# One block for all stages of a two-layer hybrid decoder, and the routers, norms and sort split by token half and by step

## The chip, the cores and the metric

The kernel runs on one core of one Trainium2 chip, as one launch. The metric is the device time of that launch in microseconds (us); lower is better. Everything is float32. Engines in the profile: PE (TensorE, with PEld for its weight loads), DVE (VectorE), ACT (ScalarE), POOL (GpSimd), SP (SyncE, which issues all DMAs; SPq is its DMA issuing).

## The reference

The input x has 256 tokens of 1024 features. Two layers, each a mixer and a mixture of experts (MoE), and a last RMSNorm:

```
h = x
for layer in 0, 1:
    u = rms_norm(h, norm_mix[layer])
    h = h + (RWKV-7 heads and sparse attention, if layer 0; Mamba-2 mixer, if layer 1)(u)
    h = h + hier_moe(rms_norm(h, norm_ffn[layer]))
return rms_norm(h, norm_final)

def hier_moe(t):                                # t: 256 x 1024
    pg = softmax(t @ wg + bg)                   # 4 groups, the best one is taken
    le = t @ we + be                            # 8 experts in each group
    e_val, e_idx = top_k(softmax(le of the group), 2)
    comb = weights of the two experts, times pg of the group
    return sum over 32 experts of comb_e * ((silu(t @ w_gate_e) * (t @ w_up_e)) @ w_down_e)
```

Each of the 32 experts has three matrices of 1024 x 512 (2 MB each). A token uses two experts, but all 32 are needed, so a layer reads 192 MB of weights.

## The kernel before, in words

`build` emits five `nc.Block`s in a row: "hyb" (mixer of layer 0), experts of layer 0, "ssm" (mixer of layer 1), experts of layer 1, "final". At the end of a block every engine waits for the others. Inside a block the engines run their own programs, written out by hand in order, and meet by counting semaphores: `then_inc(..., X.one(mark))` sets a mark and `wait_ge(*at(mark))` waits for it. `take` hands out PSUM banks in turn from a named pool and makes PE wait until the last user of that bank has been read (mark `"read", job`).

**Weights.** `raw` is a ring of 24 slots of 8 KB per partition, each holding one chunk of 1 MB: six per expert (gate and up in halves 0 to 3, down in 4 and 5). `load_ahead` (L383) issues chunks 0 to 23 as soon as the mixer's buffers that lie in the same memory are free; `main_sync` (L1762) issues the other 168, each when the chunk 24 before it has been used (semaphore `used`). Most go as whole matrices of 2 MB (`load_matrix`, L378). The first four experts are fixed to numbers 0 to 3. The order of the others comes from a sort of the experts by their token counts (`sort`, L1877, four rounds of 8 on DVE): SP waits for `order` before chunk 24 and reads the expert's number from `seq`.

**Mixer buffers.** The Areas `hyb` and `mam` lay the mixers' tensors over the ring in the order in which they come free. `hyb_fed` to `hyb_half` and `mam_projected` to `mam_left` count the slots that are free at a stage. In layer 0 they are 2, 6, 12 and 16; in layer 1 8, 12, 15, 17 and 22. The last two slots hold `hg_`, `uT_` and `junk_` of the router, and so are loaded last.

**Join.** At the end of a mixer PE multiplies its output with the output projection into four banks (two token halves t, two column halves c), and DVE adds each to h. In "hyb" (L1561 to L1578) PE does the attention part for all four tiles, then for each t transposes `mixr` (`turnr`), waits until ACT has copied it to `srcr`, and does the scan part. In "ssm" it is `joined(g)` for four groups (L2777).

**Router** (`router_sync`, `router_act`, `router_pe`, `router_dve`, L1609 to L1717). `norm_act` squares and sums h and takes the root (a table load for Exp comes behind it), `norm_dve` multiplies by the gain and builds `diag`, the identity times 1/std. PE opens the four accumulator banks with h (L1638), turns the weighted h by 16 matmuls against `diag` (`turn_pe`, L272), and once all are copied to `uT_` it computes the logits (L1647, 8 matmuls over 256 columns, 64 outputs). ACT adds the bias and writes `lgT`, PE folds it back to tokens (L1652), and three matmuls with the identity follow (L1656). DVE finds the best group and the two best experts (L1686 to L1709, `hit`), PE ranks each token within its expert and counts (L1659 to L1664), and DVE copies `rank`.

**Experts.** `select_fixed` (L1861) builds one-hot matrices for the first four experts in two operations (equal to rank, times hit), `weights_dve` and `weigh` the combine weights. Then `counts_dve` and `sort`. PE gathers the tokens (`gather_fixed`, L1968), and for each expert: project (L2014), turn, silu, down (L2052), scatter into the accumulators (L2061). A quarter of `used` is counted behind each half of project and each half of down.

**Mixer of layer 1.** `norm_act` and `norm_dve` read the accumulators `sums` in the order t = 1, 0; four matmuls with the identity run on PE; then turning (L272), copies (L281), projections (L2655, `project(n, j)`), pairs of heads (`pair`), sums of squares (`total(g)`, read by `root(g)`, L2568), all taking banks from one pool of eight. **Final** is the same norm and two outputs of 512 KB.

## Time and profile before

| | us |
|---|---|
| median of 3 runs | 1376.61 |
| lowest and highest | 1375.62, 1377.4 |
| span of the profiled execution | 1369.6 |
| its PE busy | 1239.2 (90%) |
| its DVE busy | 406.1 (30%) |
| its ACT busy | 268.7 (20%) |
| HBM read | 461.51 MB |

The span runs from the first to the last instruction of one profiled execution; the median is the device time of launches. Times in the rows count from the start of the span. PE is counted busy while matmuls are in its pipeline, also where it goes slowly, and its share is an average over stages with different limits. Stages of layer 0: mixer to 230, router to 253, experts to 678. Layer 1: mixer to 912, router to 937, experts to 1361, then the end.

### The profile page before, as it was taken

What the parts mean: (1) busy time and instruction counts of PE and PEld (TensorE: products, weight loads), DVE (VectorE), ACT (ScalarE), POOL (GpSimd) and SP (SyncE); (2) the same over time, 40 slices, a digit from 0 to 9 for tenths busy, and PEclk for the clock granted to TensorE, in tenths of its full rate; (3) what the DMA queues carried; (4) which work ended last, traced back from release to release, by engine and by line L of the source; (5) the groups of instructions that cost most, each with busy time, mean ns of one, the idle gap of its engine ahead of it and who ended that gap; (6) DMA issues with size and microseconds to landing.
All of it is one profiled execution on the core that took longest, in us unless ns stands there. A gap on an engine that the chain in (4) does not pass through costs nothing. (4 is left out here: it accounts for less than half of the span.)

```text
span 1369.6 us, 20884 instructions
## 1 busy us (share of the span) xinstructions
PE 1239.2 (90%) x8796; PEld 685.6 (50%) x8796; DVE 406.1 (30%) x1017; ACT 268.7 (20%) x537; POOL 25.5 (2%) x22
## 2 busy tenths in 40 slices
PE   6999989899999887698999999988999998877986
PEld 3678754444444333344388888444444443333432
DVE  1158963421211111021236757224212111210211
ACT  2241532110110100010222566011101100000101
POOL 0000300000000000000000011000000000000000
PEclk9999999999999999799999999999999999987999
DMA  9630158999999999999944473958999999999996
GB/s 305 193 112 13 65 218 352 405 428 428 427 427 428 427 427 427 426 426 427 361 152 169 156 277 142 418 230 328 427 428 427 427 428 427 428 427 425 428 427 260
DMA packets 63482, 464.08 MB, mean 339 GB/s; under 512 B 8272, under 2 KB 13680, under 8 KB 34960
## 3 DMA queue, kind: packets, MB, share of 16 engines
q1 hardware_dynamic: 63376, 462.61, 82.6%
q8 instruction: 73, 1.20, 0.4%
q14 instruction: 33, 0.27, 0.1%
HBM read 461.51 MB, written 1.08 MB: 338 GB/s over the span
## 5 line engine op out<-in xcount | busy, mean ns | idle before, releaser
L2014 PE MATMUL bank<-raw,xg 128*32 128x512 f32 x1664 | 234.1, 654 | 46.3 <-DMA raw<-in_moe_w_up 40.9
L1924 DVE TENSOR_TENSOR aT<-bank,sg 128x128 f32<-128x128 f32 (+1 forms) x64 | 20.2, 316 | 553.5 <-ACT sg L1835 553.5
L2014 PEld LDWEIGHTS bank<-raw,xg 128*32 128x32 f32 x1664 | 59.1, 118 | 195.6 <-issue 118.9
L1951 PE MATMUL bank<-sel,ux 128*128 128x64 f32 (+1 forms) x896 | 117.7, 287 | 17.3 <-DVE sel L1857 16.4
L1951 PEld LDWEIGHTS bank<-sel,ux 128*128 128x128 f32 x896 | 110.9, 202 | 41.0 <-issue 21.6
L2061 PE MATMUL sums<-ys,selT 64*128 64x512 f32 x512 | 127.2, 615 | 3.3 <-DVE ys L1937 3.3
L1832 ACT COPY gus<-bank 128x512 f32<-128x512 f32 x64 | 37.5, 585 | 439.4 <-PE bank L2014 331.8
L2052 PE MATMUL bank<-raw,aT 128*32 128x512 f32 x832 | 101.7, 607 | 10.7 <-DVE aT L1924 10.7
L2061 PEld LDWEIGHTS sums<-ys,selT 64*128 64x128 f32 x512 | 44.0, 186 | 88.0 <-issue 80.4
L1995 PE MATMUL bank<-raw,xg 128*64 128x512 f32 x384 | 87.3, 594 | 0.0
L2655 PE MATMUL sums<-uT,wr 128*128 128x256 f32 x352 | 78.1, 380 | 0.0
L1937 DVE COPY ys<-bank 128x512 f32<-128x512 f32 x64 | 44.0, 688 | 113.3 <-PE bank L2052 81.5
L2025 PEld LDWEIGHTS bank<-cst,gus 128*128 128x128 f32 x416 | 50.3, 191 | 44.5 <-issue 34.9
L2655 PEld LDWEIGHTS sums<-uT,wr 128*128 128x128 f32 x352 | 66.3, 190 | 9.4 <-issue 0.7
L2025 PE MATMUL bank<-cst,gus 128*128 128x64 f32 x416 | 57.5, 281 | 4.2 <-ACT gus L1832 4.2
L1806 ACT COPY xg<-bank 128x256 f32<-128x256 f32 (+1 forms) x56 | 23.4, 418 | 178.3 <-PE bank L1951 178.3
L2655 PE MATMUL bank<-uT,wr 128*128 128x256 f32 x256 | 57.1, 381 | 0.0
L1995 PEld LDWEIGHTS bank<-raw,xg 128*64 128x64 f32 x384 | 30.2, 137 | 51.5 <-issue 48.7
L2655 PEld LDWEIGHTS bank<-uT,wr 128*128 128x128 f32 x256 | 48.0, 190 | 6.9 <-issue 0.7
L2052 PEld LDWEIGHTS bank<-raw,aT 128*32 128x32 f32 x832 | 21.9, 110 | 51.3 <-issue 30.8
L2039 PE MATMUL bank<-raw,aT 128*64 128x512 f32 x192 | 43.8, 598 | 3.0 <-DVE aT L1924 3.0
L1835 ACT ACTIVATE sg<-bank 128x128 f32<-128x128 f32 (+1 forms) x64 | 19.0, 297 | 137.8 <-PE bank L2025 114.8
(419 smaller groups left out, 1260.8 us busy)
## 6 DMA issues: line engine op xcount, KB each, us to landing
raw<-in_moe_w_gate SPq DMA_DIRECT2D x54, 2048.0 KB, 41.7
raw<-in_moe_w_up SPq DMA_DIRECT2D x54, 2048.0 KB, 46.1
raw<-in_moe_w_down SPq DMA_DIRECT2D x54, 2048.0 KB, 44.7
raw<-in_moe_w_gate SPq DMA_DIRECT2D x20, 1024.0 KB, 11.6
raw<-in_moe_w_up SPq DMA_DIRECT2D x20, 1024.0 KB, 12.6
raw<-in_moe_w_down SPq DMA_DIRECT2D x20, 1024.0 KB, 12.3
wr<-in_ssm_w_in SPq DMA_DIRECT2D x10, 2048.0 KB, 8.0
wr<-in_hyb_w_in SPq DMA_DIRECT2D x5, 2048.0 KB, 7.8
```

The lines of the kernel that those rows point to most:

```text
L1806: nc.scalar.copy(dst[:, :, 4 * half:4 * half + 4, :].rearrange("p x k s -> p k x s"), bank[SIDE_BANK][:, 0:8 * n].rearrange("p (k x s) -> ...
L1832: nc.scalar.copy(gus[:, :, :], bank[GU_BANK][:, :].rearrange("p (q j) -> p j q", j=4)).then_inc(S["gus"], 1)
L1924: V.tensor_tensor(out, bank[TURN_BANK][:, 0:8 * n].rearrange("p (j x) -> p j x", j=4)[:, :, n:2 * n], gated, ALU.mult).then_inc(S["act"], 1)
L1937: V.tensor_copy(ys[:, :], bank[Y_BANK][:, :]).then_inc(S["y"], 1)
L1951: i = T.matmul(bank[SIDE_BANK][:, k * n:(k + 1) * n].rearrange("p (x s) -> p x s", x=2), ux[:, t, 4 * half + k, :], src[:, t, :, :], start ...
L1995: i = T.matmul(bank[GU_BANK][CAP * m:CAP * m + CAP, :], xg[:, odd, k, :], raw[:, slot, (k % 4) * FH:(k % 4 + 1) * FH], start=(k == 0), sto ...
L2014: i = T.matmul(bank[GU_BANK][CAP_S * c:CAP_S * c + CAP_S, :], xg_f[:, x, 4 * half + k, :], raw[:, slot, k * FH:(k + 1) * FH], start=(half ...
L2025: i = T.matmul(bank[TURN_BANK][:, j * CAP:(j + 1) * CAP], gus[:, j, :], C("ident64"), start=True, stop=True)
L2039: i = T.matmul(bank[Y_BANK][CAP * n:CAP * n + CAP, :], aT[:, j, :], raw[:, slot, jj * D + n * BANK:jj * D + (n + 1) * BANK], start=(j == 0 ...
L2052: i = T.matmul(bank[Y_BANK][CAP_S * c:CAP_S * c + CAP_S, :], aT_s[:, 2 * half + jj, :], raw[:, slot, jj * D + n * BANK:jj * D + (n + 1) * ...
L2061: i = T.matmul(bank[ACC[2 * t + n]][:, :], selT[CAP * n:CAP * n + CAP, x, t * P:(t + 1) * P], ys[CAP * n:CAP * n + CAP, :], start=False, s ...
L2655: i = T.matmul(b[:, c * SEQ:(c + 1) * SEQ], wr2[:, n % 3, k, (2 * j + c) * P:(2 * j + c + 1) * P], uT2[:, k, :], start=(k == 0), stop=(k = ...
```

## The change

1. **One block.** The five blocks become one ("all"); all waits between stages are now marks. SP's first wait of the router is for the last join tile, and of the mixer of layer 1 for the last scatter.
2. **Join.** Attention's part is done tile by tile and interleaved with the transposes of `mixr`; the `wj` weights come in one DMA. The adds to h move into the router's DVE program and write to `hn(t)`, in slot 22. The first token half is transposed (`turn_h`, plain transposes of the h that isn't normed yet) ahead of the last tile's matmuls. So in both layers.
3. **Router.** Squares in halves of 512 columns, by tile. The gain is multiplied into `rw` once by POOL (`router_weighted`), the bias is a row `rbias`, and 1/std and the bias are applied to the folded logits (`lg`) in one DVE operation per half. Logits in two groups of 128 columns. `ux` is computed from `hn` in one operation with factor and gain. The openings of the accumulators move: three between fold and rank, where the three identity matmuls were, the fourth behind rank and count, ahead of the gather. The Exp table is loaded behind the copies of `lgT`.
4. **Selection.** The table `before` has -1024 on its diagonal, so that a token not in an expert has a rank that fits no slot; `select_fixed` reads rank from PSUM in one operation per half, and `rank` is copied after it. `rexp` is waited for later, by ACT.
5. **Sort.** Two rounds, then the order of experts 4 to 15 (first count of `order`), then the weights, then the other two rounds (second count, awaited by SP before expert 16), then the overflow test.
6. **Buffers.** The first mixer's are laid out by last reading: `wr` becomes `even` and `odd`. The slots free at a stage are now 2, 4 (`hyb_scored`, behind POOL's `gain`), 7, 14 and 19. In layer 1 slot 18 is loaded when `joined(1)` is done, 15 to 17 when `joined(2)` is, and 19 to 21 at the join's end. In both layers slot 23 follows the logits, and slot 22 `ux` and the last opening.
7. **Norm into the mixer and at the end** (`sums_act`, `sums_weighted`): in halves of 512 columns, t = 0 first; the last scatter frees token half 0 by itself. Two instead of four identity matmuls. The last output of half 1 goes in two pieces, scaled by DVE and ACT.
8. **Banks at the end of the mixer of layer 1.** `project(9, ...)`, `pair(13)` to `pair(15)` and `total(2)`, `total(3)` take the four accumulator banks, the join the other four.

The diff, cut to its core:

```diff
+    entire = ExitStack()
+    block = entire.enter_context(nc.Block(name="all", no_gpsimd_drain=True))
...
-    put("before", (i[:, None] < i[None, :]).astype(np.float32))
+    put("before", (i[:, None] < i[None, :]) - MISS * np.eye(P))
...
+    def sums_act(act, tag, junk, ss, part, std):
+        for t in range(HALVES):
+            act.wait_ge(*at("h", tag, t))
+            square_act(act, sums[:, t, side(1)], junk, ss, 2 * t, "sq", tag, t, 1)
+            mean_act(act, ss, 2 * t, part, t)
+            act.wait_ge(*at("hg", tag, t, 0))
+            square_act(act, sums[:, t, side(0)], junk, ss, 2 * t + 1, "sq", tag, t, 0)
+            root_act(act, tag, ss, 2 * t + 1, part, std, t)
...
+    def turn_h(pe, tag, t, q):
+        b = take(pe, "turn", tag, t, q, pool=FREE)
+        pe.wait_ge(*at("h", tag, t, q))
+        for k in range(4):
+            i = nc.tensor.transpose(b[:, k * P:(k + 1) * P], hn(t)[:, (4 * q + k) * P:(4 * q + k + 1) * P], C("ident"))
+        i.then_inc(pe_done, PE.one(("turn", tag, t, q)))
...
+    def router_weighted(pool, layer):
+        pool.wait_ge(s_ld["rw"], 32 * (layer + 1))
+        nc.gpsimd.tensor_tensor(rw[:, :, :], rw[:, :, :], rep(FT(f"ffn{layer}"), LW, 2), ALU.mult).then_inc(
+            pool_done, PO.one(("rw", layer)))
...
+        attention_joined(0, 0)
+        attention_joined(0, 1)
+        attention_joined(1, 0)
+        scan_turned(0)
+        attention_joined(1, 1)
+        scan_turned(1)
+        pe.wait_ge(s_ld["wj"], 16)
+        scan_joined(0, 0)
+        scan_joined(0, 1)
+        scan_joined(1, 0)
+        turn_h(pe, "ffn0", 0, 0)
+        turn_h(pe, "ffn0", 0, 1)
+        scan_joined(1, 1)
...
         def router_sync(sp):
+            sp.wait_ge(*at("join", name, 1, 1))
             load_ahead(sp, layer, ahead[layer], NSLOT - 2)
+            sp.wait_ge(*at("logits", tag, 1))
+            load_ahead(sp, layer, NSLOT - 1, NSLOT)
             sp.wait_ge(*at("uhi", tag, 1))
-            sp.wait_ge(*at("logits", tag))
-            load_ahead(sp, layer, NSLOT - 2, NSLOT)
+            sp.wait_ge(*at("opened", tag))
+            load_ahead(sp, layer, NSLOT - 2, NSLOT - 1)
...
         def router_pe(pe):
+            turn_h(pe, tag, 1, 0)
+            turn_h(pe, tag, 1, 1)
+            pe.wait_ge(*at("rw", layer))
...
-                i = T.matmul(b[lo:lo + LW, 0:SEQ], rw[:, k, :], uT_[:, k, :], start=(k < 2), stop=(k >= KD - 2))
+                    i = T.matmul(b[lo:lo + LW, 0:P], rw[:, k, :], uT_[:, k, t * P:(t + 1) * P], start=(k < 2),
+                                 stop=(k >= KD - 2))
...
-            for j in range(3):
-                T.matmul(bank[GU_BANK][:, :], C("ident"), cst[:, 0:BANK], start=True, stop=True)
+            opened(0, 0)
+            opened(0, 1)
+            opened(1, 0)
             pe.wait_ge(*at("hit", tag))
...
+            opened(1, 1).then_inc(pe_done, PE.one(("opened", tag)))
...
+                go(V.scalar_tensor_tensor(out=lg[:, t, :], in0=bank_of("folded", tag)[:, t * LG:(t + 1) * LG],
+                                          scalar=rstd_[:, t:t + 1], in1=rbias[:, :], op0=ALU.mult, op1=ALU.add),
...
                     if s == FIXED:
-                        sp.wait_ge(ps.s["order"], layer + 1)
+                        sp.wait_ge(ps.s["order"], 2 * layer + 1)
+                    elif s == MIXED:
+                        sp.wait_ge(ps.s["order"], 2 * layer + 2)
...
                 select_fixed()
+                ranked_dve(dve)
+                counts_dve(dve)
+                sort(range(2))
+                order_mixed()
                 weights_dve(dve)
                 weigh(ids, plan[0] == "S")
-                counts_dve(dve)
-                sort()
+                sort(range(2, EXPERTS // 8))
+                order_small()
+                overflow()
...
-        for j in range(4):
+        for j in range(2):
             T.matmul(bank[SIDE_BANK][:, :], ident, cst[:, 0:BANK], start=True, stop=True)
...
+        project(9, 0, ACC)
+        pair(13, ACC)
+        pair(14, ACC)
+        project(9, 1, ACC)
+        pair(15, ACC)
+        total(2, ACC)
```

## Rows read from the trace of the kernel before

**Rows 1.** The page: DMA busy tenths and GB/s, 40 slices of 34.24 us

```profile
DMA  9630158999999999999944473958999999999996
GB/s 305 193 112 13 65 218 352 405 428 428 427 427 428 427 427 427 426 426 427 361 152 169 156 277 142 418 230 328 427 428 427 427 428 427 428 427 425 428 427 260
```

**Rows 2.** Stretches A:B, engines' busy us and counts, PEclk, DMA share, GB/s

```profile
core 0: us, PE busy (x) PEld busy (x) DVE busy (x) ACT busy (x) POOL busy (x), PEclk, DMA share, GB/s
250.00:253.15 3.15, 2.69 (x28) 1.65 (x24) 2.71 (x20) 0.53 (x2) 0.00 (x0) 1.00 0.99 411
300.00:400.00 100.00, 98.76 (x612) 45.12 (x604) 15.52 (x42) 11.04 (x24) 0.00 (x0) 1.00 1.01 427
670.00:674.00 4.00, 3.31 (x20) 1.36 (x23) 0.29 (x1) 1.76 (x3) 0.00 (x0) 0.70 0.43 141
690.00:837.70 147.70, 144.81 (x751) 122.11 (x750) 86.80 (x208) 70.20 (x94) 13.01 (x12) 1.00 0.50 179
```

**Rows 3.** Timeline, join of layer 0: start, us, engine, line, operation, [idle, releaser]

```profile
197.69 11.95 PE L1567 MATMUL bank<-zz,qk 128*128 128x512 f32 x24
...
212.92 0.60 PE L1173 MATMUL sums<-cst,mixr 128*128 128x128 f32 x4
213.55 0.58 ACT L1133 COPY dcy<-sums 128x512 f32<-128x512 f32 x1 [9.84 <-PE sums L1173]
...
229.61 0.69 DVE L908 TENSOR_TENSOR h<-bank,h 128x512 f32<-128x512 f32 x1 [2.74 <-PE bank L1576]
```

**Rows 4.** Timeline, router of layer 0 up to the first resumed weight load

```profile
234.21 3.73 PE L272 MATMUL bank<-diag,hg 128*128 128x128 f32 x32
...
238.67 1.95 PE L1647 MATMUL bank<-uT,rw 128*64 128x256 f32 x16 [0.72 <-issue]
240.65 0.47 ACT L1623 ACTIVATE lgT<-bank,feat 128x256 f32<-128x256 f32 x1 [2.08 <-PE bank L1647]
...
241.85 0.25 DVE L1686 MAX8 top<-bank 128x8 f32<-128x8 f32 x2 [5.22 <-PE bank L1652]
...
244.33 0.22 DVE L1709 TENSOR_TENSOR hit<-hits 128x64 f32<-128x64 f32 x1
...
244.60 0.43 PE L1659 MATMUL bank<-hit,cst 128*128 128x64 f32 x2
...
246.06 0.43 DVE L1865 TENSOR_TENSOR sel<-sel,hit 128x256 f32<-128x256 f32 x1
...
246.64 2.47 PE L1968 MATMUL bank<-sel,ux 128*128 128x128 f32 x20 [0.95 <-DVE hits L1727]
...
249.12 1.92 PE L2014 MATMUL bank<-raw,xg 128*32 128x512 f32 x16
...
251.99 0.17 DVE L1893 CAST seq<-ranked 128x16 int32<-128x16 uint32 x1
...
253.15 0.36 SPq L380 DMA_DIRECT2D raw<-in_moe_w_gate  x1
```

**Rows 5.** Timeline, layer 1: last join add, first resumed weight load

```profile
912.00 0.69 DVE L2511 TENSOR_TENSOR h<-sums,h 128x512 f32<-128x512 f32 x1 [2.74 <-PE sums L2784]
...
937.28 0.34 SPq L380 DMA_DIRECT2D raw<-in_moe_w_gate  x1
```

**Rows 6.** Timeline, end of layer 0 and start of the mixer of layer 1

```profile
676.00 1.99 PE L2061 MATMUL sums<-ys,selT 64*128 64x512 f32 x8 [0.82 <-DVE ys L1937]
...
682.11 3.78 PE L272 MATMUL bank<-diag,front 128*128 128x128 f32 x32
...
686.62 0.67 PE L2708 MATMUL sums<-uT,wr 128*128 128x256 f32 x2 [0.72 <-issue]
```

**Rows 7.** Timeline, late mixer: project(9, 0) on PE and root(1) on ACT

```profile
838.25 7.07 PE L2655 MATMUL sums<-uT,wr 128*128 128x256 f32 x32
838.45 0.47 ACT L2568 ACTIVATE rs<-sums,eps_n 128x256 f32<-128x256 f32 x1 [0.43 <-PE sums L2692]
```

**Rows 8.** Timeline, final norm and output, in a span of 1369.6

```profile
1361.23 1.02 ACT L232 ACTIVATE junk_f<-sums 128x1024 f32<-128x1024 f32 x1 [4.18 <-PEq L2125]
...
1365.12 1.20 SPq L295 DMA_DIRECT2D out<-o_f  x2
```

More of the change, by code:

```diff
@@ L1349, in _, with against @@
+        by_channels(5, NV, 0)
+        scores(1)
+        def against(name, left_):
+            for t in range(HALVES):
+                bs = [take(pe, name, t, e, pool=right) for e in range(2)]
                 for c in range(4):
@@ new lines, in _ @@
+                        if t == 1 and c == 3 and q == 1:
+                            i.then_inc(pe_done, PE.one(("nn", e)))
+        by_channels(5, NV, 1)
+        weights_turned(0)
+        pe.wait_ge(*at("rt"))
+        against("bar", bh)
+        bs = [take(pe, "crossed", e, pool=right) for e in range(2)]
+        for c in range(4):
+            for e in range(2):
+                for q in range(2):
+                    i = T.matmul(bs[e][at64(1 - q), c * CHK:(c + 1) * CHK],
+                                 bh[at64(e), c, chunk(1, q)], ar[at64(e), c, 0, chunk(1, q)], start=True, stop=True)
@@ new lines, in _, with products @@
+        straight = lambda g, q: q
+        crossed = lambda g, q: q if g == 0 else 1 - q
+        def products(l):
+            pe.wait_ge(*at("lvl", l))
+            if l == 1:
+                pe.wait_ge(*at("triT0"))
+            else:
+                pe.wait_ge(*at("read", "dT", l - 1, 1))
+            bs = {g: take(pe, "prod", l, g, pool=right) for g in range(2)}
+            squares(bs, lv[:, l % 2], tri, straight, crossed).then_inc(pe_done, PE.one(("prod", l, 1)))
+            new[("prod", l, 0)] = new[("prod", l, 1)]
@@ new lines, in _ @@
+        pe.wait_ge(*at("read", "dTT", LAST, 1))
+        for e in range(2):
+            bs = [take(pe, "wu", t, e, pool=right) for t in range(HALVES)]
+            for c in range(4):
+                for q in range(2):
+                    for t in range(HALVES):
+                        half = at64(crossed(t, q))
+                        i = T.matmul(bs[t][at64(q), 2 * c * CHK:2 * (c + 1) * CHK], triT[half, slot(t, e, c), :],
+                                     flat(xr_[half, slot(t, e, c), :, :], "x", "s"), start=True, stop=True)
+            i.then_inc(pe_done, PE.one(("wu", 1, e)))
+            new[("wu", 0, e)] = new[("wu", 1, e)]
@@ L1447, in _, with within @@
+        def within(t):
+            b = take(pe, "y", t, pool=right)
             for e in range(2):
```

3131 lines of the change are left out of this document (1581 added, 1550 removed).

## The prediction

> **What bounds the kernel now.** I read the page's row of slices first. The DMA engines are full in two long stretches, at 425 to 428 GB/s [rows 1], and in each the kernel streams the expert weights of one layer. A layer has 192 chunks of 1,048,576 bytes. The ring holds 24, so 168 chunks (176.2 MB) can start only once slots are freed: 412 us at 427 GB/s [rows 2]. In the stretch 300 to 400 us PE is 98.8% busy, but so is the DMA, and what PE does faster only empties the ring earlier. So the end of a layer is fixed by the moment at which the stream resumes after the first 24 chunks, plus about 420 us. That moment is the DMA issue at 253.15 in layer 0 and at 937.28 in layer 1 [rows 4, 5]. Whatever lies ahead of it counts fully; whatever lies behind it is hidden.
>
> The second reading is the timeline from the last output projection ("join") to that issue. In layer 0 the last add to h starts at 229.61, so I call J = 229.57 the end of the join on PE [rows 3]; the stream resumes 23.6 us later. In layer 1 J is 911.96 [rows 5] and the distance 25.3 us. These two stretches are serial chains: block change, norm, 16 turning matmuls, logits, bias, fold, picking of experts, rank, select, gather, first half of an expert [rows 4]. The DMA is still busy at 250 to 253 in layer 0 at nearly full rate [rows 2], so there the chunk loads finish only just ahead of the issue: a shorter router alone would soon hit them.
>
> Third, the mixer of layer 1 is PE's: 144.8 of 147.7 us busy at clock 1.00 [rows 2]. It takes as long as it did, moved earlier as a whole. Fourth, the end: norm and output, serial [rows 8].
>
> **The change, part by part.**
>
> *Join of layer 0.* Before, PE waited twice for a copy out of PSUM between transposing mixr and using it: four transposes from 212.92, then the copy of 0.58 at 213.55 [rows 3], about 0.65 in which PE has nothing. Now attention's and scan's matmuls are interleaved, and others cover both waits: -1.3. Two groups of raw transposes for the router (four take 0.60 [rows 3], about 0.5 back to back) are put ahead of the last output tile: +1.0. The 32 matmuls of 512 columns and the transposes of mixr stay. J comes at 229.3, 0.3 earlier; bounds 1.3 earlier and 1 later.
>
> *Router, from J to the issue.* By the new order, in us after J. The last add, 0.04 + 0.69 [rows 3]: 0.75. Four raw transposes of that tile, 0.60 [rows 3]: 1.35; the other twelve lie before it. Its copy to uT on DVE, priced as the add (512 columns out of PSUM, 0.69): 2.1. The logits are now two groups of 8 matmuls over 128 columns; the old one, over 256 columns, took 1.95 [rows 4]. Half is 1.0; I take 1.15 each, for the weight loads don't shrink. The first starts at 1.35 and the second follows: 3.65. The copy of its half of lgT, 0.3 (256 columns took 0.47 [rows 4]): 4.0. The fold of that half, 0.4: 4.4. Two multiply-adds with factor and bias, new, 0.4 with the wait behind them: 4.8. From the first MAX8 to hit it was 241.85 to 244.55 [rows 4], 2.7: 7.55. Rank and count on PE, then the fourth accumulator opening, which stands ahead of the gather: 0.9 and 0.88 (512 columns at the rate of 16 matmuls of 256 in 7.07 [rows 7]): 9.4. The selection needs two operations instead of copy and two, ends at 8.9, and is no longer what the gather waits for. Gather to first expert matmul, 246.64 to 249.12: 2.5, and half an expert, 1.92 [rows 4]: 13.8. Freed slot to issue: 13.85.
>
> What would have held the issue in the old order is the sort: its last cast is at 251.99, the issue 1.15 later [rows 4], although the slot was free at 251.04. Now two of four rounds are enough: about 3.0 us of DVE behind the selection, then 1.0 for the register: 12.9. That is cover with 0.9 us to spare. The squares, roots and the ux multiplication of the second half run beside transposes, logits and fold (DVE is idle from 2.1 to 4.4 but for them); without that cover they would cost 1.3. The three other openings (2.6 us) run on PE while DVE picks the experts, where before three identity matmuls ran. SP: in layer 0, slots 0 to 18 (before: 0 to 15) are issued before J. Five chunks follow J (12.3 us at 2.45) instead of eight from 230.66. The last, slot 22, is issued at 9.4, so it lands by about 13.4: also just in time. The added bias row and rw's second semaphore count are waited for long after they land; POOL's product of rw and the gain runs while POOL has nothing else, in layer 0 behind its last operation of that stage, in layer 1 ahead of xdt, which waits for the first group of channels.
>
> So from J to the issue 13.85 instead of 23.6 (layer 0) and 25.3 (layer 1, where the old block end also waited for SP to issue five chunks). Bounds: 13.0, if the opening falls beside something; 17, if halves cost as much as the wholes did. Gains: 9.75 + 0.3 = 10.05 in layer 0 and 11.5 in layer 1.
>
> *Into the mixer.* The last scatter runs 676.00 to 677.99, the turning matmuls start at 682.11, the projections at 686.62 [rows 6]. Now the first token half is released 1.0 earlier and no block ends. The squares are in halves: four instead of two, on ACT the chain from 677.05 to about 681.35 (0.77 each with the read of the sum, from the 0.58 of a 512-wide ACT operation in rows 3, and 0.3 for each small one, both estimates). Turning of half 0 starts at 679.8. ACT's copies then end at 684.4 and not 686.5: -2.1. Bounds 0.5 and 3.
>
> *Inside the mixer.* The late banks are taken from two pools. By counting what each pool has handed out, project(9,0) gets the bank of total(1), which root(1) reads. It started at 838.25, and that read at 838.45 lasts 0.47 [rows 7]: +0.7. Bounds 0 (other count) and 3 (a table load in between). The two groups of router transposes ahead of the last tile: +1.0. PE is full there, so both count: +1.7. Slot 18 and slots 15 to 17 are loaded a stage earlier than their like; DMA has room (slices of 142 to 277 GB/s [rows 1]).
>
> *End.* First square at 1361.23, first output at 1365.12, span 1369.6 [rows 8]. Starting on the first half during the scatter, no block change, halves at the end split between DVE and ACT, and output pieces of 256 KB behind the second inverse: the last issue at about 1365.1 instead of 1366.0, its landing somewhat shorter: -1.7. Bounds 0.5 and 3.
>
> Sum: -10.05 - 2.1 - 11.5 + 1.7 - 1.7 = -23.65. The span goes from 1369.6 to 1345.95. The median of the runs shown, 1376.61, stands 7.0 above the span of the profiled execution; I keep that distance: 1353.0.
>
> *A rule against it.* The sixteen turning matmuls of each router, 3.73 us of ordinary matmuls [rows 4], become transposes. At the router's end (250 to 253) the granted clock is 1.00, 2.4 GHz; where PE waited for the last weights (670 to 674) it is 0.70 on average, a mix of the 1.2 and 2.4 GHz levels [rows 2]. The Trainium skill ("TensorE: Matmul & The Clock Gate", Part 4: PE-mode transpose) says that transposes don't count as activity for the clock as matmuls do. No row here tells that apart, since each group of four stands between matmuls. By the rows the router stays at full clock; by the rule it may not, which is the first rival.
>
> **Rivals.**
> 1. *Clock low in both routers.* PE's share of the 13.85 us: transposes 0.6, logits 2.3, fold 0.4, rank to opening 1.8, gather 2.0, half expert 1.9, together 9.0. At 1.2 GHz each doubles: +9.0 twice, 1371.0. For: identity matmuls are taken out. Against: 2.6 us of opening matmuls take their place, and before J PE is full with 512-column matmuls. This is also where the page's rule leads.
> 2. *Part of the chain is longer than summed*, 17 us: ACT serves squares, copies and roots in a fixed order, or the sort or slot 22 ends later than the freed slot. +3.15 in each layer: 1359.3. For: three ends lie within 1 us of each other, so any of them late decides. Against: each operation has a row.
> 3. *Slower than before: the mixer at low clock.* The four identity matmuls ahead of its turning become two, after the waits of 670 to 674. Each us of mixer work at 1.2 GHz costs 1 us. It decides from 23.65 + 2.8 = 26.4 us of such work; with 40 us the time is 1393.0. Against: 144.8 us of nearly unbroken matmuls at clock 1.00 [rows 2]; the low clock would have to outlast them.
> 4. *The stream isn't freed early*: chunk loads in layer 0 run at the old rate into 250, and layer 0 gains only 2 of its 10: 1353.0 + 8 = 1361.0. Against: three chunks more lie ahead of J.
>
> **How the numbers follow.** My forecast 0.70, rival 2 0.13, rival 4 0.05, rival 1 0.06, rival 3 0.02, no effect at all 0.02 (the parts cancel), 0.02 for a gain beyond 28 us. The bounds of the unknown costs give 1348 to 1360; the range takes in rivals 2 and 4: 1347.5 to 1362. A measurement of this kernel can tell about 0.2%, 2.8 us, from no change. Faster 0.95, same 0.03, slower 0.02.
>
> **What would show it.** Right: first resumed chunk 13 to 15 us after the last join add begins, in both layers, and behind the first half expert rather than the casts; the slots all landed by then; stream at 427 GB/s afterwards; mixer projections about 8.5 us after the last scatter begins; one PE wait of 0.7 behind root(1); last output issued some 6.5 us after the last scatter begins. Wrong: clock below 1.00 between J and the issue; DMA idle over 2 us ahead of the issue, with PE waiting on ACT; a new PE wait in the join or the mixer above 1 us; the stream below 425 GB/s.

## The result and the profile after

The kernel after takes 1352.68 us, the median of 4 runs (1351.68 to 1354.93), against 1376.11 us (1371.72 to 1377.40) for the kernel before in the same session: ratio 0.9838, 95% interval 0.9823 to 0.9853, 23.4 us less. The forecast was 1353.0 and 23.65 us less. The profiled execution took 1352.72 us, with a span of 1350.9. One run of e1 below, in which the chip stood in a slower state (2057.23 us at a mean granted clock of 0.552), is left out of its median.

The page of the kernel after, the rows that answer to [rows 1] (slices of 33.77 us), with PEclk:

```profile
PEclk9999999999999988799999999999999999987989
DMA  9621149999999999999964464879999999999996
GB/s 299 193 77 63 65 173 414 404 428 427 427 428 427 428 425 428 424 428 427 375 209 172 156 230 191 357 276 406 426 430 426 426 427 427 428 426 426 426 429 286
```

The two stretches at 427 GB/s are still there, as long as before. To see where the time went I cut both spans at the same events:

| stretch | before | after | forecast | measured |
|---|---|---|---|---|
| start to last join add, layer 0 | 229.61 | 234.99 | -0.3 | **+5.38** |
| last join add to resumed issue, layer 0 | 23.54 | 14.00 | -9.75 | -9.54 |
| resumed issue to last scatter, layer 0 | 422.85 | 422.34 | 0 | -0.51 |
| last scatter to mixer's projections | 10.62 | 8.26 | -2.1 | -2.36 |
| projections to last join add, layer 1 | 225.38 | 227.20 | +1.7 | +1.82 |
| last join add to resumed issue, layer 1 | 25.28 | 13.96 | -11.5 | -11.32 |
| resumed issue to last scatter, layer 1 | 421.37 | 421.37 | 0 | 0.00 |
| last scatter to end of span | 10.95 | 8.78 | -1.7 | -2.17 |
| span | 1369.6 | 1350.9 | -23.65 | -18.70 |

Seven of eight stretches came out within 0.6 us of the forecast. The first is off by 5.7 us, and it lies before nearly everything that the change was priced for. It gets its own section below. The -0.51 of the third row is no gain of the change: in the profile before, the clock was low during part of the last expert, which took 11.92 us from one scatter to the next, against 10.26 in the profile after (more on this at e3).

Timeline of the kernel after, router of layer 0, from the last join tile to the resumed issue, which answers to [rows 3, 4] (start, us, engine, line, operation, idle before it and who ended it):

```profile
233.93 1.02 PE L1631 MATMUL bank<-odd,dcy 128*128 128x512 f32 x2
...
234.99 0.69 DVE L1780 TENSOR_TENSOR hg<-bank,h 128x512 f32<-128x512 f32 x1 [2.95 <-PE bank L1631]
...
235.83 0.63 PE L321 MATMUL bank<-cst,hg 128*128 128x128 f32 x4 [0.44 <-DVE hg L1780]
...
236.38 1.97 PE L1736 MATMUL bank<-uT,rw 128*64 128x128 f32 x32
...
237.29 2.09 DVE L1788 SCALAR_TENSOR_TENSOR ux<-hg,rstd,gain 128x1024 f32<-128x1024 f32 x1
...
238.28 0.85 PE L1742 MATMUL bank<-cst,lgT 128*128 128x40 f32 x4
...
238.96 2.82 PE L1750 MATMUL sums<-hg,cst 128*128 128x512 f32 x6
...
239.29 0.43 DVE L1805 SCALAR_TENSOR_TENSOR lg<-bank,rstd,rbias 128x40 f32<-128x40 f32 x2
...
239.75 0.24 DVE L1810 MAX8 top<-lg 128x8 f32<-128x8 f32 x2
...
242.20 0.23 DVE L1833 TENSOR_TENSOR hit<-hits 128x64 f32<-128x64 f32 x1
...
243.40 1.10 PE L1750 MATMUL sums<-hg,cst 128*128 128x512 f32 x2
...
244.34 2.39 PE L2116 MATMUL bank<-sel,ux 128*128 128x128 f32 x20
...
246.18 0.16 DVE L2029 CAST seq<-ranked 128x4 int32<-128x4 uint32 x1
...
246.85 1.92 PE L2162 MATMUL bank<-raw,xg 128*32 128x512 f32 x16
...
248.99 0.36 SPq L434 DMA_DIRECT2D raw<-in_moe_w_gate  x1
```

J is 234.95 here and the issue comes 14.04 us later (forecast 13.85). No block ends between them, and nothing stands between the last add and the transposes. The last needed cast is at 246.18, well before the half expert ends at 248.77: the freed slot now releases the stream, not the sort, as forecast. Layer 1 repeats it: last add at 906.79, resumed issue at 920.75.

The stretches of the kernel after around the router of layer 0, and the mixer of layer 1 (columns as in [rows 2]):

```profile
235.00:242.50 7.50, 6.34 (x51) 3.89 (x49) 6.30 (x25) 4.21 (x13) 0.00 (x0) 1.00 1.01 407
242.50:249.00 6.50, 6.38 (x48) 4.36 (x49) 5.33 (x32) 1.93 (x4) 0.00 (x0) 1.00 1.00 410
249.00:252.00 3.00, 2.54 (x24) 1.54 (x27) 2.48 (x17) 0.92 (x3) 0.00 (x0) 1.00 0.89 317
679.60:831.40 151.80, 148.87 (x772) 125.55 (x772) 87.55 (x209) 70.51 (x94) 14.05 (x13) 1.00 0.54 191
```

DMA is busy up to the issue and dips to 0.89 just behind it: the fixed load of the first 24 chunks and the router now end together. The granted clock is 1.00, its 2.4 GHz level, through the whole router and the mixer.

The last rows of after are the way into the mixer, the wait for the bank, and the output; they answer to [rows 6 to 8]:

```profile
671.33 1.99 PE L2209 MATMUL sums<-ys,selT 64*128 64x512 f32 x8 [0.81 <-DVE ys L2085]
...
672.50 0.60 ACT L231 ACTIVATE front<-sums 128x512 f32<-128x512 f32 x1 [2.78 <-PE sums L2209]
...
679.59 0.67 PE L2860 MATMUL sums<-uT,wr 128*128 128x256 f32 x2 [0.72 <-issue]
...
832.08 1.10 PE L2807 MATMUL sums<-uT,wr 128*128 128x256 f32 x4 [0.66 <-ACT rs L2720]
...
1342.12 1.99 PE L2209 MATMUL sums<-ys,selT 64*128 64x512 f32 x8 [0.81 <-DVE ys L2085]
...
1346.26 2.32 SPq L333 DMA_DIRECT2D out<-o_f  x3
```

The first square starts 1.17 us behind the scatter's begin, while its second half still runs. The wait of 0.66 us behind root(1) is the forecast one.

### The profile page after: what moved, and what is told of

It reads as the page before. It is cut to its first block, busy times and chain, and to the rows that moved or that the text cites. A ratio compares the mean times of both kernels' runs of the same rounds, so it can differ in the third digit from the quotient of the medians.

```text
span 1350.9 us, 20836 instructions
## 1 busy us (share of the span) xinstructions
PE 1229.3 (91%) x8780; PEld 678.1 (50%) x8780; DVE 405.4 (30%) x1019; ACT 272.1 (20%) x562; POOL 27.6 (2%) x24
## 4 chain that ended last, share of the span: by engine, by line
PE 61%; DMA 25%; DVE 7%; ACT 3%; issue 2%; another core or an unknown queue 1%; SPq 0%; DVEq 0%; ACTq 0%
DMA raw<-in_moe_w_gate 14%; PE bank L2162 10%; DMA raw<-in_moe_w_up 9%; PE bank L2143 6%; PE sums L2807 5%; PE sums L2209 5%; PE bank L2099 5%; PE bank L2939 4%; PE bank L2200 4%; PE bank L2807 3%; PE bank L2187 3%; PE bank L2173 2%; DMA even<-in_hyb_w_in 2%; PE bank L1207 2%; PE bank L1216 2%
## 5 line engine op out<-in xcount | busy, mean ns | idle before, releaser
L2807 PE MATMUL sums<-uT,wr 128*128 128x256 f32 x384 | 85.4, 381 | 0.7 <-ACT rs L2720 0.7
L2807 PEld LDWEIGHTS sums<-uT,wr 128*128 128x128 f32 x384 | 72.2, 190 | 11.3 <-issue 1.9
L1937 ACT COPY xg<-bank 128x256 f32<-128x256 f32 (+1 forms) x56 | 23.4, 418 | 177.3 <-PE bank L2099 177.3
L2143 PEld LDWEIGHTS bank<-raw,xg 128*64 128x64 f32 x384 | 27.3, 137 | 51.9 <-issue 50.9
L2807 PE MATMUL bank<-uT,wr 128*128 128x256 f32 x224 | 49.9, 381 | 0.0
L2200 PEld LDWEIGHTS bank<-raw,aT 128*32 128x32 f32 x832 | 21.7, 109 | 50.6 <-issue 30.4
L2807 PEld LDWEIGHTS bank<-uT,wr 128*128 128x128 f32 x224 | 42.0, 190 | 5.9 <-issue 0.5
```

Source lines behind the costliest of these rows:

```text
L2143: i = T.matmul(bank[GU_BANK][CAP * m:CAP * m + CAP, :], xg[:, odd, k, :], raw[:, slot, (k % 4) * FH:(k % 4 + 1) * FH], start=(k == 0), sto ...
L2200: i = T.matmul(bank[Y_BANK][CAP_S * c:CAP_S * c + CAP_S, :], aT_s[:, 2 * half + jj, :], raw[:, slot, jj * D + n * BANK:jj * D + (n + 1) * ...
L2807: i = T.matmul(b[:, c * SEQ:(c + 1) * SEQ], wr2[:, n % 3, k, (2 * j + c) * P:(2 * j + c + 1) * P], uT2[:, k, :], start=(k == 0), stop=(k = ...
```

## The experiments

Eleven more runs were made: nine variants of the kernel after or before (e2 to e10), and the kernel after unchanged, twice (e1, e11). The distance from last join add to resumed issue repeats to 0.04 us in all profiles that leave the router as it is (13.96 to 14.00); the stretches with a clock dip in them, a short time in which TensorE is granted its lower clock, repeat less well. The times of whole runs settle only about 0.2% (3 us), so most verdicts below rest on the stretches. "Issue" is the distance from last join add to resumed issue in layers 0 and 1.

| run | median us | ratio to before, 95% | issue, us | span |
|---|---|---|---|---|
| e1 after again | 1351.39 | 0.9825 [0.9799, 0.9851] | 13.99, 13.97 | 1350.3 |
| e2 one block undone | 1355.36 | 0.9856 [0.9831, 0.9882] | 14.00, 13.98 | 1354.9 |
| e3 sort in one step | 1354.43 | 0.9834 [0.9808, 0.9860] | 13.99, 13.97 | 1353.6 |
| e4 before, sort in two | 1373.57 | 0.9987 [0.9972, 1.0003] | 22.15, 23.84 | 1371.3 |
| e5 router delayed | 1360.56 | 0.9908 [0.9890, 0.9926] | 19.15, 19.11 | 1358.8 |
| e6 stream delayed | 1353.78 | 0.9844 [0.9816, 0.9872] | 13.98, 13.97 | 1352.4 |
| e7 turn after norm | 1358.13 | 0.9880 [0.9862, 0.9899] | 17.21, 17.20 | 1356.4 |
| e8 bias late | 1351.32 | 0.9838 [0.9822, 0.9854] | 13.99, 13.98 | 1350.9 |
| e9 buffers moved | 1348.98 | 0.9813 [0.9790, 0.9835] | 14.00, 13.98 | 1351.7 |
| e10 three edits | 1348.42 | 0.9819 [0.9796, 0.9842] | 13.52, 13.51 | 1343.2 |
| e11 after, control | 1351.41 | 0.9822 [0.9798, 0.9846] | 13.99, 13.98 | 1353.2 |

### Does the moment of the issue set the end?

e5, one delay in the router, and e6, the same delay in the stream:

```diff
 # e5
             opened(1, 1).then_inc(pe_done, PE.one(("opened", tag)))
+            for _ in range(6):
+                T.matmul(bank[SIDE_BANK][:, :], C("ident"), cst[:, 0:BANK], start=True, stop=True)
 # e6
                     pe.wait_ge(S["gus"], b0 + e + 1)
+                    if closes and t == 2 and not odd:
+                        for _ in range(6):
+                            T.matmul(bank[TURN_BANK][:, :], C("ident"), cst[:, 0:BANK], start=True, stop=True)
                     turned(small)
```

> Six more matmuls of 512 columns between the last opening and the first gather of each router (their bank is cleared by the gather that follows; nothing is left out). An opening of this form takes 0.94 us here (three in 2.82 us), so the gather starts 5.1 to 5.6 us later. Theory of the prediction (the chain from the last join tile to the first freed slot sets the time one for one): restart of the stream 5.1 to 5.6 us later in each layer (19.3 us behind the last join addition in place of 14.0), and 10.2 to 11.2 us more in all (about 1363). Rival (part of the chain is slack that the stream makes up while it waits for TensorE in the first experts): the restart moves as much, but the stretch from restart to last scatter shrinks, 0 to 7 us more in all.

> The same six matmuls, but within each expert stage, in the third pair behind its middle (its bank is cleared by the turning behind them; nothing is left out). Theory (there the stream of weights sets the time and TensorE waits for it, 17 us of idle in 130 us before the last experts): no more time, the stretch from restart to last scatter stays at 421 to 422 us in both layers; the 5.1 to 5.6 us vanish in TensorE's waits for the weights. Rival (TensorE is as long as the stream, a delay frees slots late and the queue runs dry): up to 5.6 us more in each layer, 11 us in all.

The two delays as the timelines of e5 (router of layer 0) and e6 (expert stage of layer 0) show them:

```profile
243.10 5.31 PE L1766 MATMUL bank<-cst 128*128 128x512 f32 x12
...
252.91 0.36 SPq L434 DMA_DIRECT2D raw<-in_moe_w_gate  x1
```

```profile
624.37 5.42 PE L2248 MATMUL bank<-cst 128*128 128x512 f32 x12
```

In the router the delay moves the issue by 5.16 and 5.14 us against e1. Issue to last scatter stays (421.27 and 421.15 us; it is 421.03 to 422.6 in the runs that change neither the sort nor the stream). The run gets 9.2 us longer than e8's on the same chip (1360.56 against 1351.32), where the two delays add up to 10.3; the difference is within what the times can tell. In the stream 5.4 us of extra work on PE vanish: 422.05 and 421.18 us, as in the kernel after. Behind the last scatter of layer 0, e6 needs 10.14 us to the projections in place of 8.26, at a mean clock of 0.57 from 668 to 676; e7, which has no such edit, needs 9.99 there, at 0.59, so this is the clock. e6's median, 2.5 us above e8's, rules out a price of 11 us but not a small one; the stretches do. The theory holds: work ahead of the issue counts one for one, this much work in the middle of the stream not at all.

### The parts of the router

e4 gives the kernel before the two-step sort alone; e3 takes it out of the kernel after.

```diff
 # e3: kernel after
-                sort(range(2))
+                sort(range(EXPERTS // 8))
                 order_mixed()
+                order_small()
                 weights_dve(dve)
                 weigh(ids, plan[0] == "S")
-                sort(range(2, EXPERTS // 8))
-                order_small()
 # e4: kernel before
-                sort()
+                sort(range(2))
+                order_mixed()
+                sort(range(2, EXPERTS // 8))
+                order_small()
```

(In e4 SP waits for `order` at 2 * layer + 1 at the first ordered expert and at 2 * layer + 2 at the first small one, as in the kernel after.)

> The kernel before with nothing changed but the sort in two steps. Theory (its stream restarts 1.16 us behind the last cast of the order; without the last two rounds, 1.9 us, the order is there at 250.1 us and the half expert's projection ends at 251.0 us): restart 1.9 us earlier in each layer, 3.8 us faster in all, ratio 0.9972. Rival (the restart doesn't set the end, because TensorE falls behind the stream in the first experts): 0 to 1 us faster.

> All four rounds of the sort run before the first order is given, and the routing weights behind them. Theory (the half expert's projection, 248.77 us in the first layer, now sets the restart of the stream; the order came 1.9 us ahead of need and would now be ready at 248.2 us, with 1.2 us of register reading behind it): the restart slips by 0.4 us in each layer, +0.8 us in all (1353.5). Rival A (the sort is still what ends last): +1.9 us in each layer, +3.8 us (1356.5). Rival B (the weights, 1.9 us later, hold up TensorE in the first expert and the slots behind it): also up to +3.8 us, but with the restart only 0.4 us later.

Timeline of e4, then of e3, layer 0:

```profile
232.97 0.69 DVE L908 TENSOR_TENSOR h<-bank,h 128x512 f32<-128x512 f32 x1 [2.74 <-PE bank L1576]
...
253.95 0.16 DVE L1897 CAST seq<-ranked 128x4 int32<-128x4 uint32 x1
...
255.12 0.36 SPq L380 DMA_DIRECT2D raw<-in_moe_w_gate  x1
```

```profile
247.91 0.17 DVE L2033 CAST seq<-ranked 128x16 int32<-128x16 uint32 x1
...
249.32 0.36 SPq L434 DMA_DIRECT2D raw<-in_moe_w_gate  x1
```

In e4 the issue comes 1.39 and 1.44 us earlier, not 1.9: two rounds are shorter than I had taken. The last cast that SP waits for begins 1.17 us ahead of the issue, as in the kernel before (1.16), so the sort goes on setting it. That is 2.8 us for both layers, and the time can't tell it from nothing. In e3 the order is complete at 248.08, only 1.24 us ahead of the issue, and the issue has not moved at all (13.99). So my +0.4 was wrong and so was rival A. Both runs say the same: the sort set the issue only in the old order; in the new one it ends early enough to have no effect, except as cover that must not be eaten. By itself the two-step sort gave the kernel before 2.8 us; taken out of the kernel after, it loses none of the 21 us that both routers gained.

e3's span is 3.3 us above e1's all the same, behind the issue: its streams take 423.23 and 422.83 us, against 421.03 to 422.43 and 421.10 to 422.56 in the other profiles derived from after. Two rows of its layer 1 show where that comes from, the second half of the last expert and the window around it:

```profile
1340.67 3.34 PE L2199 MATMUL bank<-raw,aT 128*32 128x512 f32 x16 [0.69 <-DVE aT L2071]
```

```profile
1338.00:1346.00 8.00, 5.82 (x33) 2.25 (x32) 0.98 (x2) 2.38 (x5) 0.00 (x0) 0.79 0.19 79
```

The same 16 matmuls take 1.92 us in e1, at clock 1.00. Up to the scatter before the last one, e3's streams take 411.48 and 411.17 us, and the others derived from after 410.52 to 412.07 and 410.61 to 411.41. The last expert, from one scatter to the next, takes 11.75 and 11.67 us in e3. Over both layers of all thirteen profiles it is 10.24 to 10.28 us where the clock was 1.00 in it (14 times) and 11.13 to 11.92 where it wasn't (12 times). e3 had such a dip in both layers, as e7 and e9, which leave the sort alone, have. So rival B (the weights, 1.5 us later, hold up TensorE) is out as well: the 3.3 us are clock.

e7 makes the transposes wait for the norm again:

```diff
+            pe.wait_ge(*at("rstd", tag, 1))
             turn_h(pe, tag, 1, 0)
             turn_h(pe, tag, 1, 1)
```

(`inverse` of half 1 goes ahead of DVE's copy, and ACT's copy behind the root, so that neither waits for the other.)

> In each router the transposes of the second half wait until the norm of that half is known, as in the kernel before; the factor still goes onto the folded logits. Theory (transposing raw rows gives the path the time in which squares, root and reciprocal are worked out): transposes begin behind the reciprocal, 2.4 us later than now (237.2 in place of 234.8 us), DVE's share of the copies and the 2.1 us of the scaled rows come behind them, and the restart slips by 2.1 us in each layer, +4.2 us in all (about 1357). Rival (the norm and the scaled rows on DVE end last in any case, the transposes are beside them): the restart slips by under 0.7 us in each layer.

Timeline of e7, layer 0, and its windows over both routers:

```profile
231.81 0.69 DVE L1781 TENSOR_TENSOR hg<-bank,h 128x512 f32<-128x512 f32 x1 [2.95 <-PE bank L1631]
...
233.61 0.16 DVE L268 RECIPROCAL rstd<-std 128x1 f32<-128x1 f32 x1 [1.11 <-ACT std L242]
...
233.83 1.62 PE L321 MATMUL bank<-cst,hg 128*128 128x128 f32 x8 [2.06 <-DVE rstd L268]
...
235.38 3.06 PE L1737 MATMUL bank<-uT,rw 128*64 128x128 f32 x32
```

```profile
232.00:240.00 8.00, 6.15 (x47) 5.05 (x48) 4.00 (x8) 3.36 (x7) 0.00 (x0) 0.79 1.01 415
906.00:916.00 10.00, 7.91 (x51) 5.61 (x50) 3.99 (x7) 3.32 (x8) 0.00 (x0) 0.83 0.69 263
```

The issue slips by 3.2 us in each layer, half as much again as the theory gave. PE waits 2.06 us, and behind that wait the clock is down to 0.79 and 0.83 over these windows: the 32 logits matmuls take 3.06 us in place of 1.97. In this profile the wait costs itself and a dip, in both routers; in the routers of after and of its other variants, which have no such wait, the clock is 1.00. So not waiting for the norm, which the factor on the folded logits makes possible, is worth 6.4 us of the 21, and the time shows it (1358.13 against 1351.32 in e8 on the same chip; the intervals of the ratios don't meet). The rest, 12 to 14 us depending on whether the 2.8 of the sort are taken off, is the block end, the two halves, fewer copies, the fused selection and the openings in place of identity matmuls together; I didn't take these apart, since the block end between join and router can't be put back without moving the transposes that PE issues within the join.

### The block ends behind the scatters

e2 closes the block and opens the next one ahead of the second mixer and ahead of the final norm.

```diff
+    entire.close()
+    entire = ExitStack()
+    block = entire.enter_context(nc.Block(name=name, no_gpsimd_drain=True))
```

> The block is closed and opened again behind the scatter that ends each expert stage (before the second mixer and before the final norm); the split norms stay. Theory (all engines wait at a boundary for the last matmul, so the first half can't start under the second half of the scatter): first square 2.6 us behind the scatter's begin as in the kernel before, against 1.17 us now, so +1.4 us at each boundary, +2.8 us in all (about 1355.5). Rival (the gain there comes from the norm in four pieces alone and the boundary costs only its own 0.6 us once the scatter is done): under +1.2 us in all.

e2, ACT's first square after the scatter of layer 0 (which begins at 671.30):

```profile
673.88 0.60 ACT L238 ACTIVATE front<-sums 128x512 f32<-128x512 f32 x1 [4.18 <-PEq L158]
```

2.58 us behind the scatter's begin in place of 1.17. Scatter to projections is 9.67 us (8.27 in e1), scatter to end 10.01 (8.83): +1.40 and +1.18, or 2.6 where the theory gave 2.8 and the rival under 1.2. Most of what the change gained there is the block end. Another 1.7 us of e2's span is a clock dip in the mixer, which e8 and e11 have too (below).

### The start, where the forecast failed

e8 tests the row of biases (`load_bias` is the line taken out of `load_router`), e9 where the weight buffers lie.

```diff
 # e8
     def load_router(sp, layer):
 ...
-        load(sp, "rw", rbias[:, :], row_src(f"rb{layer}"))
+        if layer:
+            load_bias(sp, layer)
 ...
+        load_bias(sp, 0)
         sp.wait_ge(*at("gup", 1))
 # e9
+    hyb.at += 64
     even = hyb("even", [P, 4 * D])
```

> The changed kernel once more, beside the next three on one chip, as the base for what they add. Forecast 1352.7 us again, 0.984 of the kernel before. Its trace decides a question left open by the first one: there the changed kernel reached its first join 6.1 us later than the profiled kernel before (203.76 against 197.69 us), with a granted clock of 0.89 between 70 and 102 us. If the changed start (the row of biases loaded early, the four norm and weight loads behind it) costs this, the join begins near 203.8 us again; if it was the clock of that one execution, it begins near 198 to 199 us.

> The first layer's row of biases (4.3 us of issue on SP's queue, 18.2 to 22.5 us) is loaded behind the last group of the first mixer's weights, not ahead of the third group. Theory (it pushes back the loads queued behind it, and TensorE waits 1.4 us longer for the third group's weights than in the kernel before): the first mixer's join begins 1 to 1.5 us earlier, the first addition at about 222.3 us in place of 223.6 to 224.2, and 1.2 us less in all (1351). Rival (the later start of the join, 2.2 to 6 us against two profiles of the kernel before, is TensorE's clock in the first 140 us alone): the wait for the third group stays or the join begins at 223.6 us again.

> The two weight buffers of the first mixer (and what lies behind them) start 64 bytes further up in SBUF, so that they begin at a multiple of 128 bytes, as the ring of the kernel before did; nothing else is changed. Theory (the loads into them run at 388 GB/s in place of 406 to 410 between 12 and 20 us, and land 2.8 us later than in the kernel before, because of where the buffers lie): the rate in that stretch is back at 406 or more, the wait of 1.5 to 2.0 us for the third group's weights goes, and the join begins 1.5 us earlier. Rival (the rate comes from something else, such as where the weights lie in HBM): 388 GB/s again, the waits stay, and the time is that of the changed kernel.

Windows of 12 to 20 and 80 to 108 us: e4 (whose start is that of the kernel before), then e11, then e9 (PE busy, PEclk, DMA share, GB/s):

```profile
12.00:20.00 8.00, 6.36 (x32) 1.00 1.05 409
80.00:108.00 28.00, 26.49 (x132) 0.82 0.37 141
```

```profile
12.00:20.00 8.00, 6.09 (x30) 1.00 1.05 390
80.00:108.00 28.00, 26.45 (x140) 0.88 0.42 151
```

```profile
12.00:20.00 8.00, 6.56 (x29) 1.00 1.05 406
80.00:108.00 28.00, 26.45 (x135) 0.82 0.41 149
```

PE at the third group's weights, e11 then e9 (e4 has no wait there, the profile before one of 0.25):

```profile
45.73 2.63 PE L1207 MATMUL bank<-even,uT 128*128 128x280 f32 x10 [1.23 <-DMA even<-in_hyb_w_in]
```

```profile
45.01 3.33 PE L1208 MATMUL bank<-even,uT 128*128 128x280 f32 x13 [0.31 <-DMA even<-in_hyb_w_in]
```

The 5.4 us have two causes.

*First, the clock.* The profile before that I worked from has clock 1.00 from 80 to 108 us; e4, whose code there is the same, has 0.82, and its first join add is at 221.36, not 218.00. Those 3.4 us are no work of the change. e1, which was to decide between clock and changed start, couldn't: its join began at 203.93, which by its own rule spoke for the start, but its clock from 80 to 108 was 0.82 too.

*Second, the loads.* The last join add of after is 2.0 us behind e4's (234.99 and 232.97); in e8 and e11 it is 1.5 us behind, and 1.7 to 1.8 us are there by 53 us. The biases aren't it: in e8 the wait for the third group stays (1.06 us), and its last join add is where e11's is (234.50). The place of the buffers is a part. In the nine profiles with the buffers of after, the loads run at 390 to 391 GB/s from 12 to 20 us and the third group's matmuls begin at 45.61 to 46.28; in the two with the buffers 64 bytes further up (e9, e10) it is 406 GB/s, and 45.01 and 44.91. PE is 0.7 us earlier at 53 us in e9 than in e11, and the last join add 1.0 us, where the theory gave 1.5.

What is left can be told at equal clock. e10 (below) has e9's start and the clock of the profile before, 1.00 from 80 to 108. First join add of before, then first and last of e10:

```profile
218.00 0.69 DVE L908 TENSOR_TENSOR h<-bank,h 128x512 f32<-128x512 f32 x1 [9.79 <-PE bank L1576]
```

```profile
218.11 0.69 DVE L1782 TENSOR_TENSOR hg<-bank,h 128x512 f32<-128x512 f32 x1 [9.00 <-PE bank L1633]
...
229.29 0.69 DVE L1782 TENSOR_TENSOR hg<-bank,h 128x512 f32<-128x512 f32 x1 [2.96 <-PE bank L1633]
```

The last add is 0.3 us ahead of that of before (229.61), although the join's first matmul comes 1.3 us later (198.98 against 197.69). The pair at low clock, e9 and e4, has the same 1.3 us there (202.60 against 201.26) and ends 0.5 us behind. And e9 is 4.2 us behind e10 at the last add, on the same code up to there: that is the clock alone. So with the buffers moved the whole stretch is as long as before within 0.5 us. The 1.3 us ahead of the join are unexplained; 0.4 to 1.1 of them are there by 53 us, where before and e4, with the same code, differ by 0.65 among themselves.

### Three edits more

```diff
 # e10, with e9's edit
             opened(1, 0)
+            opened(1, 1).then_inc(pe_done, PE.one(("opened", tag)))
 ...
-            opened(1, 1).then_inc(pe_done, PE.one(("opened", tag)))
 ...
+    LATE = (5, 6, 7, 4)
 ...
-        project(9, 0, ACC)
+        project(9, 0, LATE)
```

(and LATE in the calls of `pair`, `project` and `total` behind it.)

> The moved buffers and two edits more. The fourth opening of each router goes ahead of the wait for the hits, with the other three (TensorE sits idle there for 0.7 us, and the opening's 0.94 us now lie ahead of the first gather): the restart comes 0.4 us earlier in each layer (13.6 us behind the last join addition). The late work of the second mixer takes its banks in the order 5, 6, 7, 4, so that the projection (9, 0) doesn't wait for the root in the bank: the 0.7 us of wait goes and the stretch from the first projection to the last join addition is 226.5 us. In all 1.5 us less, 3.0 us if the moved buffers bring their 1.5 us (1349.5). Rival (the openings delay the counts of the hits as much as they save, and the projection waits for the next bank in its place): nothing from both.

> The changed kernel once more as the base for the two runs ahead of it, on the same chip: 1352 us, restarts 14.0 us behind the last join additions, first join addition at 223.6 us if four dips of TensorE's clock fall before it, 1.7 us less for each dip fewer.

Timeline of e10, late mixer and layer 0's router:

```profile
824.31 0.70 PE L2846 MATMUL sums<-sq,cst 128*128 128x256 f32 x2
824.84 3.40 PE L2809 MATMUL sums<-uT,wr 128*128 128x256 f32 x15
```

```profile
233.26 3.68 PE L1752 MATMUL sums<-hg,cst 128*128 128x512 f32 x8
...
242.81 0.36 SPq L435 DMA_DIRECT2D raw<-in_moe_w_gate  x1
```

The projection follows the total without a wait, and projections to last add take 226.25 us (227.2). All four openings fit in ahead of the hits, whose first matmul begins 7.49 us behind the last add (7.50 in after), and the issue comes at 13.52 and 13.51: 0.47 us gained in each layer. These (0.94 and 0.93 us) and the 0.7 of e9 add up to 2.6 us. The median is 3.0 us below that of e11 (1348.42 and 1351.41) and 0.6 below that of e9 (1348.98), but the intervals of the ratios overlap, so by time alone it isn't shown that e10 beats the kernel after; by the stretches it does. Its short span of 1343.2 is in part the clock of the profiled execution, 0.969 on average against 0.961 in e11.

## Why the prediction was right, and where it wasn't

**Bound.** Right, and shown. Everything rests on the sentence that the resumed issue sets the end of a layer; e5 and e6 tested it from both sides.

**Join of layer 0**, forecast -0.3. From its first matmul (203.76, before at 197.69) to the last add it took 31.23 us, 0.69 less (0.85 less from e4 to e9, 1.6 from before to e10). The gain was there, rather larger than forecast; what was missing was any term for the stretch in front of it. I gave the re-laid buffers no term at all, and they cost 1.0 to 1.3 us at the last add (233.46 in e9 against 234.50 in e11 and 234.76 in e1); 1.3 us more ahead of the join I can't explain. The added bias row I did price at nothing, and e8 bears that out. And I took the profiled clock of the first 140 us as a property of the kernel, where it was that of one execution: 3.4 to 4.2 us.

**Router**, forecast 13.85 us from J in both layers, measured 14.04 and 14.00. Within it, logits were cheaper (both groups 1.97 us, forecast 2.3) and the scaled rows dearer: `ux` takes 2.09 us, ends at 239.38, when the folded logits have been ready for 0.25 us, so that the multiply-adds start at 239.29, 4.34 after J (forecast 4.4). DVE really was full there, so that cover is used up. The cover for the sort was wider than the 0.9 us I gave it: 1.4 us later, in e3, it still held nothing up. The opening ahead of the gather, which I said held it, did, by 0.47 us (e10; the forecast had 0.5 between the two).

**Into the mixer**, -2.1, measured -2.36, of which e2 puts 1.4 on the block end. **Mixer**, +1.7, measured +1.82: the wait for root(1) was 0.66 where 0.7 was forecast, from counting what each pool hands out. **End**, -1.7, measured -2.17, of which 1.2 is the block end.

**Rivals.** Rival 1 (low clock in the routers) didn't happen: 1.00 from 235 to 249. That speaks for weighing rows above the rule of the Trainium skill ("TensorE: Matmul & The Clock Gate", Part 4: PE-mode transpose) that transposes don't count as activity the way matmuls do, as long as they are few among matmuls: the eight nearest J take 1.2 us in all. But in e7, with eight transposes behind a wait of 2.06 us, the clock did go down, in both routers. Whether the wait or the transposes did it, that run can't tell. Rival 2 (a chain of 17 us) is what e7 became. Rival 3 (mixer at low clock) didn't happen; where a dip does fall into the mixer it costs 1.7 us, far from the 26.4 that would decide. Rival 4 is out: the issue in layer 0 came 14.00 us behind the last add, as early as in layer 1, with DMA at 407 to 410 GB/s up to it.

**From span to median.** I kept 7.0 us between them. 1.8 of that is fixed (1352.72 - 1350.9). The other 5.2 were no property of the kernel. Part was the clock of the profiled execution, whose 1369.6 + 1.8 = 1371.4 us lie 2.9 below 1374.3, the median of all 41 runs of before; the rest is that the median of three runs that I started from, 1376.61, lies 2.3 above it. The span came out 5 us above the forecast and the median on it. That the absolute time was hit to 0.3 us is luck: a distance that I kept without explaining it stood for the dips and the slow start that the next profile showed. The forecast of what the change is worth owes less to it. Compared at equal mean clock (0.961 to 0.963), 11 runs of before average 1374.5 and 7 of after 1352.7: 21.7 us. The stretches behind the first add up to -24.1, and with +1.5 to +2.0 from the start (e8, e11, e1 and after against e4) to -22.1 to -22.6. All 41 runs of before and 15 of after have medians of 1374.3 and 1351.7, 22.7 apart. The true gain is some 22 to 23 us, where 23.65 was forecast.

## What to carry to other kernels

Where a long stream of loads sets the time, find the one instruction that resumes it, sum the chain up to it in the new order, and price everything behind it at nothing; then look for which of two or three near ends holds it, because what isn't the latest costs nothing (e3 makes the sort 1.4 us later for free) and shortening the latest gains only down to the next (e10 takes an opening of 0.94 us out of the chain and gains 0.47). Before you read a distance off one profile, check the granted clock of every stretch it spans. And give a term to every buffer that moves, even one that no line of the argument uses.

## What was new about the hardware

- **Clock dips cost steps of 1.7 us.** Windows of 8 us around a single dip show 0.79: 232 to 240 in e7, 696 to 704 in e8, 700 to 708 in e2. That is 1.7 us of full-speed work. Others are twice that: 0.57 from 132 to 140 in after and from 1340 to 1348 in e11. A stretch full of PE work is so either its usual length or 1.7 us longer: from the mixer's projections to the last add it is 227.15 to 227.31 us in seven profiles of after and its derivatives and 228.84 to 228.98 in three. Why these three have a dip in a mixer in which PE is busy throughout isn't shown. The runs' spans follow: over 37 runs of before the span falls by 0.7 us for each 0.001 of mean clock.
- **Where in SBUF a load goes can set its rate.** With rows of 2 KB or less, buffers that begin 64 bytes past a multiple of 128 took 390 to 391 GB/s between 12 and 20 us (nine profiles), and 406 at a multiple of 128 (e9, e10; 409 in before and e4, also at a multiple of 128). e9 moves all that lies behind these buffers too, and only this one distance was tried. The stream's larger pieces run at 427 GB/s although their ring begins 32 bytes past a multiple of 64, so this is not so for every load.
- **A multiply-add over a transposed view is dear.** `ux` (1024 columns, both tensors that it reads taken with a stride of 8 elements within a row) takes 2.09 us on DVE. Two other operations of the same kind and size in the kernel after, whose tensors lie in order (L773 and L799), take 1.23 and 1.22 us. They differ in a second way, a constant in place of a factor for each row. The kernel before has a pair without that difference: a plain product of 1024 columns with the factor of a row takes 1.15 us over the transposed view (L1681) and 0.75 us in order (L262).
